# A decoder layer on one core: a quarter of the expert blocks' first layer moves beside the gate tables, and the window copies move forward

## The reference, cut to what matters

```python
def peer_ffn(x, wq, subkeys, u_tab, v_tab):          # x: 544 tokens of 1024
    q = (xi @ wq).reshape(PEER_TOKEN_BLOCK, PEER_HEADS, 2, PEER_DKEY // 2)
    s = jnp.einsum('nhcd,ckd->nhck', q, subkeys)      # 2 x 128 scores per head
    sv, si = lax.top_k(s, K)
    ...
    g = jax.nn.softmax(top_s, axis=-1)
    hpre = jnp.einsum('nd,nhkd->nhk', xi, u_tab[eid])
    a = jax.nn.gelu(hpre, approximate=False) * g
    return jnp.einsum('nhk,nhkd->nd', a, v_tab[eid])
...
kc = jnp.concatenate([state_k_win, kd_s], axis=1)     # k_win_sample: the window buffer moved on by 4 rows
vc = jnp.concatenate([state_v_win, vd_s], axis=1)
```

## Time and profile before

| | |
|---|---|
| median of 3 runs | 2651.59 us (2644.68 to 2654.73) |
| the profiled execution | 2648.93 us; its span 2647.1 us, mean granted clock 0.917 |
| busy over the span | PE 2289.9 us (87%), DVE 1610.1 (61%), ACT 928.9 (35%), POOL 359.4 (14%) |
| chain that ended last | PE 68%, DVE 10%, DMA 5% |
| transfers | 555 MB, mean 210 GB/s |

### The profile page before, as it was taken

The page is one execution under the profiler, slowest core; times in us unless marked ns, Lnnn a source line. Parts: engine busy times, 40 slices in busy tenths (PEclk is TensorE's granted clock), DMA queues, the critical chain, the costliest instruction groups (busy, mean ns, idle before and its releaser), DMA issues.

```text
span 2647.1 us, 38437 instructions
## 1 busy us (share of the span) xinstructions
PE 2289.9 (87%) x13177; PEld 1955.8 (74%) x13177; DVE 1610.1 (61%) x3159; ACT 928.9 (35%) x1417; POOL 359.4 (14%) x370
## 2 busy tenths in 40 slices
PE   7997879998997989504376999999999999999994
PEld 7996656666664469503376999999999999999993
DVE  3433322343434347799994667777677776777767
ACT  3225533444445122102263333333333333333331
POOL 0000000000000000100000223222232222322230
PEclk9998879899988989856687999999999999999997
DMA  3220026667665111299965888888787887878873
GB/s 121 91 73 33 1 91 200 201 207 225 198 201 190 64 48 49 80 323 339 364 263 201 278 274 283 275 281 278 272 284 275 282 278 273 285 273 282 278 273 105
DMA packets 214837, 555.47 MB, mean 210 GB/s; under 512 B 16993, under 2 KB 87202, under 8 KB 212066
## 3 DMA queue, kind: packets, MB, share of 16 engines
q1 hardware_dynamic: 165730, 315.16, 36.3%
q0 software_dynamic: 49024, 239.23, 25.4%
HBM read 521.95 MB, written 98.83 MB: 235 GB/s over the span
## 4 chain that ended last, share of the span: by engine, by line
PE 68%; DVE 10%; DMA 5%; SPq 2%; ACT 2%; issue 1%; POOLq 0%; DVEq 0%; ACTq 0%; POOL 0%
PE psum L1913 20%; PE psum L1925 19%; PE psum L1523 4%; PE psum L1903 4%; DMA gates_dram<-gate_table 3%; PE psum L978 3%; PE psum L1386 3%; PE psum L1050 2%; PE psum L1032 2%; DVE gate_table L1726 2%; PE psum L968 2%; PE psum L1000 2%; DMA sample<-in_cache_v_sb_dram 2%; DVE gate_table L1723 1%; PE psum L1766 1%
## 5 line engine op out<-in xcount | busy, mean ns | idle before, releaser
L1913 PE MATMUL psum<-h_parts,expert_parts 128*128 128x384 f32 x3072 | 592.9, 341 | 4.2 <-DVE expert_parts L2013 4.2
L1925 PE MATMUL psum<-expert_parts 128*128 128x512 f32 x2304 | 557.2, 395 | 0.0
L1913 PEld LDWEIGHTS psum<-h_parts,expert_parts 128*128 128x128 f32 x3072 | 537.7, 189 | 14.6 <-DVE expert_parts L2013 4.8
L1925 PEld LDWEIGHTS psum<-expert_parts 128*128 128x128 f32 x2304 | 423.3, 188 | 83.5
L2013 DVE TENSOR_TENSOR expert_parts<-psum,expert_parts 128x512 fp32r<-128x512 f32 x256 | 177.1, 692 | 293.2 <-ACT expert_parts L1955 293.2
L1961 ACT ACTIVATE expert_parts<-peer 128x1024 fp32r<-128x1024 f32 x128 | 135.8, 1061 | 365.9 <-PE psum L1925 365.9
L1955 ACT ACTIVATE expert_parts<-psum 128x512 fp32r<-128x512 f32 x256 | 153.1, 598 | 200.5 <-PE psum L1903 200.5
L2053 DVE SCALAR_TENSOR_TENSOR kept<-experts,kept 128x1024 f32<-128x1024 f32 x160 | 204.7, 1280 | 3.9 <-DVE kept L2043 2.8
L1305 DVE TENSOR_TENSOR sample_parts<-sample,sample_parts 128x512 fp32r<-128x512 f32 x128 | 85.2, 690 | 158.0 <-ACT sample_parts L1158 158.0
L394 PE MATMUL psum<-projection_parts 128*128 128x256 f32 (+1 forms) x1440 | 173.7, 282 | 3.8 <-DVE projection_parts L500 3.8
L1883 POOL DMA_INDIRECT experts<-in_peer_u_dram,kept x96 | 113.0, 1178 | 468.5 <-DVE experts L2037 345.4
(11 more groups left out here) (271 smaller groups left out, 2993.7 us busy)
## 6 DMA issues: line engine op xcount, KB each, us to landing
peer<-in_peer_u_dram SPq DMA_DIRECT2D x128, 512.0 KB, 5.6
peer<-in_peer_v_dram SPq DMA_DIRECT2D x128, 512.0 KB, 3.7
sample<-in_cache_k_sb_dram SPq DMA_DIRECT2D x128, 256.0 KB, 3.1
sample<-in_cache_v_sb_dram SPq DMA_DIRECT2D x128, 256.0 KB, 3.0
out_dram<-in_state_k_win_dram POOLq DMA_DIRECT2D x8, 4088.0 KB, 104.9
out_dram<-in_state_v_win_dram POOLq DMA_DIRECT2D x8, 4088.0 KB, 118.2
gates_dram<-gate_table SPq DMA_DIRECT2D x12, 2048.0 KB, 8.4
experts<-gates_dram SPq DMA_DIRECT2D x32, 768.0 KB, 6.0
```

Of the source, the lines that this page charges most:

```text
L1913: last = pe.matmul(bank(6)[:, 0:ND], lhsT=u_t[s][:, a, k, :], rhs=h1_r[:, b, k, 0:ND], start=(k == 0 and n == 0), stop=(k == KD - 1 and n ...
L1925: last = pe.matmul(bank(2 * t + half), lhsT=weight[s][:, a, t * P:(t + 1) * P], rhs=v_r[s][:, b, half * 512:(half + 1) * 512], start=(firs ...
```

## The change

1. **Early blocks.** Of every four expert blocks the last (block 4e+3, 32 in all) has its first layer computed in the gate-table stage, from the whole f32 tokens (`h1_f`, written by ACT in the norm stage by one more copy for each of six half tiles) and whole f32 `u`: per early block 8 transposes and 8 f32 matmuls on PE, two copies and a gelu on ACT, a load of 512 KB and a store of 192 KB (`gelu_dram`) on SP. Psum banks 6 and 7 hold them, so the table quarters go round three pairs of banks where they had four. 12 early blocks stand ahead of the first `turn`, 5 ahead of the second, 5 ahead of the third, and 10 inside chunks.
2. **Experts.** A block with k % 4 == 3 has no `turn_u`, `hidden` or `activate`; its gelu is loaded (L1996 of the changed kernel). SP issues the next `u` load ahead of the `v` load.
3. **Window copies.** The 16 copies are issued 7 in prompt attention (behind `counts_in`), 4 in dilated attention, 3 in the norm stage, 2 in the query stage.
4. **No barrier behind the queries**, and the query halves are 384 and 256 tokens wide instead of 320 each. The chunk loops of PE, ACT and SP are written out instead of looped.

```diff
+        MOVES = (7, 4, 3, 2)
+        def move_state(pool, turn):
+            for n in range(sum(MOVES[:turn]), sum(MOVES[:turn + 1])):
...
+                pool.dma_start(to[b].rearrange("w h d -> (w h d)")[0:(WIN - DT) * DH],
+                               frm[b].rearrange("w h d -> (w h d)")[DT * DH:WIN * DH]).then_inc(sem("window_moved"), 16)
...
         @part("pool")
         def _(pool):
+            pool.wait_ge(sem("counts_in"), 2 * 16)
+            move_state(pool, 0)
             pool.wait_ge(sem("v_sb_out"), 2 * 16)
...
+                    if t < NTD:
+                        act.activation(h1_f[:, 4 * half:4 * half + 4, t * P:(t + 1) * P],
+                                       bank(4 + u % 4).rearrange("p (k n) -> p k n", k=4), ACT.Copy)
...
-        for engine in programs:
-            programs[engine].append(end_stage)
...
+        EXP_AFTER = {1: 0, 5: 1, 10: 2, 15: 3, 22: 4}
+        BLOCK_OF = {1: 17, 2: 18, 3: 19, 4: 25, 5: 26, 6: 27, 7: 28, 8: 29, 9: 30, 10: 31}
+        FIRST_OF = ((0, 12), (12, 17), (20, 25))
+
+        def gate_schedule(turn, block, chunk):
+            for t in range(NTD + 1):
+                if t < NTD:
+                    for e in range(*FIRST_OF[t]):
+                        block(e)
+                    turn(t)
+                if t >= 1:
+                    for c in range(TILE_CHUNKS * (t - 1), TILE_CHUNKS * t):
+                        chunk(c, BLOCK_OF.get(c))
...
+            def hidden_early(e, half):
+                pe.wait_ge(sem("early_copied"), 2 * e + half + 1)
+                if half == 0 and e >= 1:
+                    pe.wait_ge(sem("early_gelu"), e)
...
+                for k in range(4 * half, 4 * half + 4):
+                    last = pe.matmul(bank(6)[:, 0:ND], lhsT=early_t[e % 2][:, k, :], rhs=h1_f[:, k, :],
+                                     start=(k == 0), stop=(k == KD - 1))
...
+            def block_half(e, half):
+                turn_early(e + 1, half)
+                hidden_early(e, half)
...
+            def exponents(e):
+                if e in EXP_AFTER:
+                    act.wait_ge(sem("best_less"), EXP_AFTER[e] + 1)
                     act.activation(gate_e, gate_e, ACT.Exp).then_inc(sem("gate_exp"), 1)
...
-                    for half in range(2):
-                        hidden(x, s, half)
-                        if not is_last(turn, k):
-                            turn_u(x + 1, 1 - s, SET * turn + (k + 1) // 2, half)
+                    if is_full(k):
+                        j = full_of(k)
+                        f = FULL * turn + j
+                        for half in range(2):
+                            hidden(f, j % 2, half)
+                            if not is_last(turn, k):
+                                turn_u(f + 1, 1 - j % 2, FULL // 2 * turn + (j + 1) // 2, half)
                     if not (isinstance(turn, int) and turn == 0 and k == 0):
                         add_up(x - 1, 1 - s, first=isinstance(turn, int) and turn == 0 and k == 1)
```

More of the change, by code:

```diff
@@ L681, in build, with _ @@
         assert place[0] <= WORK + 6 * WIDE
+        @part("pool")
+        def _(pool):
+            move_state(pool, 1)
         @part("pe")
@@ L1484, in top16, with _ @@
                 st.wait()
+        @part("pool")
+        def _(pool):
+            move_state(pool, 3)
         @part("sp")
@@ L1671, in build @@
         hot_i = [take(HALF_C * NK).rearrange("p (n i) -> p n i", n=HALF_C) for _ in range(2)]
[L1673 to L1677, removed]
+        early_gelu = [take(ND) for _ in range(2)]
+        early_t = [take(D).rearrange("p (k j) -> p k j", k=KD) for _ in range(2)]
         def columns(x, c, half, first=0, n=HALF_C):
@@ L1758, in turn, with turn_early @@
                 last.then_inc(sem("ijg_turn"), 1)
-            def spread(c, s, i):
+            def turn_early(e, half):
+                if e == SETS:
+                    return
+                if half == 0:
+                    pe.wait_ge(sem(f"early_in_{e % 2}"), 16 * (e // 2) + 16)
+                pe.wait_ge(sem("early_copied"), 2 * e + half)
+                for k in range(4):
+                    last = pe.transpose(bank(7)[:, k * P:(k + 1) * P], early_u[e % 2][:, 4 * half + k, :], ident)
+                last.then_inc(sem("early_turned"), 1)
@@ L1771, in _ @@
-            for t in range(NTD + 1):
-                if t < NTD:
-                    turn(t)
-                if t >= 1:
-                    pe.wait_ge(sem("ijg_turned"), min(t + 1, NTD))
-                    over_chunks(pe, t - 1, spread)
+                    for q in range(2 * half, 2 * half + 2):
+                        r = 4 * c + q
+                        pe.wait_ge(sem("table_copied"), r + 1)
+                        for n in range(QUARTER):
+                            at = q % 2 * QUARTER + n
+                            last = pe.matmul(bank(2 * (r % 3) + n // 4)[:, n % 4 * NK:(n % 4 + 1) * NK],
+                                             lhsT=hot_j[half][:, at, :], rhs=hot_i[half][:, at, :], start=True, stop=True)
+                        last.then_inc(sem("table_ready"), 1)
@@ L1778, in _ @@
+                    if e is not None:
+                        block_half(e, half)
+            turn_early(0, 0)
+            turn_early(0, 1)
+            gate_schedule(turn, block, chunk)
         @part("act")
         def _(act):
-            act.drain().then_inc(sem("table_copied"), 4)
+            act.drain().then_inc(sem("table_copied"), 3)
             act.drain().then_inc(sem("table_out_0"), 16)
             act.drain().then_inc(sem("table_out_1"), 16)
-            def copy(c, s, i):
-                act.wait_ge(sem(f"table_out_{s}"), 16 * i + 16)
-                for q in range(4):
-                    act.wait_ge(sem("table_ready"), 4 * c + q + 5)
-                    act.activation(table[s][:, :, 8 * q:8 * q + 8].rearrange("p i n -> p n i"),
-                                   bank(2 * q, 2).rearrange("p (n i) -> p n i", n=8), ACT.Copy).then_inc(sem("table_copied"), 1)
@@ L1804, in build @@
+            copy_early(0, 0)
+            copy_early(0, 1)
+            gate_schedule(turn, block, chunk)
+            gelu_early(SETS - 1)
         for engine in programs:
```

225 lines of the change are left out of this document (156 added, 69 removed).

## The result

The changed kernel takes **2499.9 us** (median of 4 runs, 2498.9 to 2501.6) where the kernel before took 2650.1 beside it: a ratio of 0.9435, 95% interval 0.9415 to 0.9454. The forecast was 2517 us, the range 2488 to 2560. The profiled execution took 2500.06 us, its span 2498.3, where 2647.1 stood before.

What follows compares the result with a forecast made beforehand. PE was taken to bound the experts, DVE the gate tables. Terms -160 + 1 + 5 + 19 + 1 = -134 us took the span from 2647.1 to 2513; adjusted to the median, 2517 us, range 2488 to 2560.

Steps and rivals of the forecast that it cites:

- experts: Expert stage: 32 blocks lose `hidden` and `turn_u`, 5.00 us each, if PE stays the bound: -160 us.
- gate tables: Gate tables: PE's early blocks fit nearly beside DVE's work, and copies no longer crowd table stores: +1 us, bounds -3 and +10.
- prompt attention, POOL's drain: Prompt attention: POOL's drain waits for seven copies, so the barrier opens at about 309 instead of 304: +5 us.
- norm stage: Norm stage: norm rows land only when three copies end, so PE stops 18 us, plus 1 for clock: +19 us.
- queries: Query stage: two copies hold the next piece of weights until about 981, some 6 us late: +1 us, bounds 0 and +6.
- rival C: Experts: the shortened block starves as `v_low` or its inputs come late: +16 to +48 us, 2533 to 2565; chance 0.12.
- SP gets 12 of its 16 turns while the copies last: Norm stage: queues alternate packet for packet, so the norm rows land when the copies end, about 911.5 to 912.5 us.
- Rival A: Norm stage: the norm rows are not held up by the copies, 19 us less, 2498 us; chance 0.17.
- The copies no longer crowd the table stores: Gate tables: DVE's 2.7 us wait for ACT, held up by a late-landing store, goes.
- The missing barrier gives no time: Start of the gate tables: DVE sets the pace and went straight on at 1110, so dropping the barrier gains nothing.
- 7 - 2.5 = 4.5 us: Gate tables, chunks 4 to 10: PE falls 7 us behind DVE; the double buffer of one-hot factors hides 2.5.
- Rivals B and D: Gate tables, PE's clock low: B at 0.76, +76 us, 2592, chance 0.10; D at 0.5 throughout, +268, 2785, chance 0.03.

Runs made afterwards that it cites:

- x6: The kernel before with the window copies moved 7, 4, 3, 2 and nothing else changed: 2665.1 us, ratio 1.0053.
- x5: The changed kernel with the barrier behind the queries put back: 2512.7 us, ratio 0.9479.
- x10: The changed kernel with the barrier back, ACT's first exponential ahead of the early blocks and the next three exponentials three early blocks earlier: 2508.5 us.
- x1: The changed kernel with six window copies in prompt attention and five in dilated attention: 2498.4 us, ratio 0.9428.
- x2: The changed kernel with POOL waiting for the norm's two rows before it issues the norm stage's three copies: 2491.1 us, ratio 0.9383.
- x3: The changed kernel with the norm's rows issued some 5 us later, behind two memsets of DVE, copies unmoved: 2515.4 us.
- x8: The changed kernel with copies split 6, 4, 5, 1 and those of the norm stage behind the norm's rows: 2479.7 us, ratio 0.9353.
- x4: The changed kernel with all 16 window copies in the gate tables again, early blocks kept: 2647.2 us, ratio 0.9991.

## Why the prediction was right, and where it was not

The forecast was right in sign and by its main term. Its sum was -134 us against -148.8 measured:

| term | forecast | measured | shown by |
|---|---|---|---|
| experts | -160 | -165.1 | changed, x6 |
| gate tables | +1 | -1.5 | x5, x6, x10 |
| prompt attention, POOL's drain | +5 | +6.4 | x1 |
| norm stage | +19 | +9.4 | x2, x3 |
| queries | +1 | +3.4 | x6, x8 |
| up to 204 us, dilated, sample, end | 0 | -1.4 | unedited |

**Experts.** The mechanism held: PE stayed the bound without a gap, so rival C did not come about. A block was 5.11 us cheaper, not 5.00: two runs of `add_up` that follow each other take 8.27 us (1911.24 to 1919.51) instead of 2 x 4.19; 32 x 5.11 = 163.5, and the rest is the stage's start, where PE's longest wait before the loop is 1.5 us instead of 2.7.

**Norm stage.** The mis-sized term. The step "SP gets 12 of its 16 turns while the copies last" took the two queues to start together. They share one for one, as I had read from the earlier trace rows, but half of the 256 row packets had gone before the copies' packets came. With the rows issued 5.6 us late the stage cost +22.8 (x3: 104.9 against 82.1); less those 5.6 us it is some 17 (an estimate), near the 19 of the forecast. Rival A's 2498 us is near the time by chance only: its premise, rows not held up, is false, since taking the hold away gives 9 us (x2).

**Gate tables.** Near in sum by luck: three parts were mis-sized, and they cancel. "The copies no longer crowd the table stores" was taken as 2.7 us and is 7.1 (x6). "The missing barrier gives no time" is false: it gives 12.8 us (x5), as PE's head start, and without it PE would hold DVE (x10). Of the early blocks themselves I had 7 - 2.5 = 4.5 us; with the barrier in place they cost 323.9 - 305.5 = 18.4 (x5 against x6), and only with the head start 5.6. PE's own work was sized well, 279 us busy where I had 281; what DVE pays for it was not. Rivals B and D did not come about: PE's longest wait in the stage was 4.8 us, and the clock was 0.96 to 0.98.

**Prompt attention and queries.** The drain ends when the copies do, as read from the earlier trace rows; the cost was 1.4 us larger. In the queries ACT waited for the late piece of weights, and PE for the low parts, 6.2 us instead of 3.7:

```profile
ACT wq_parts L1576 <- DMA peer<-in_peer_wq_dram: 10.9, 1, 10.9
...
PE psum L1562 <- DVE wq_parts L1610: 6.2, 2, 3.7
```

My estimate had the two copies end at 981 on the old time scale and PE covered by its pieces in hand; the cover was too thin by some 2 us, inside the bound of 6. The copies alone cost 1.2 us here (x6, halves of 320), and the new halves without the wait cost nothing (x8, 156.8 us against 157.1); why both together cost 3.4 is open.

## What to carry to other kernels

Work that moves off the engine that bounds a stage is worth its whole time if that engine stays without gaps, and its price lies where it goes. Look whether the engine there still has slack once the moved work is in; if not, a barrier ahead of it or an operation behind it on a third engine (here ACT's exponentials) becomes the price. A bulk copy was free here beside work that waits for no transfer (dilated attention took 69.0 to 71.3 us with four or five copies in it, 70.6 and 71.3 without) and dear beside small loads that something waits for: let the issuing engine wait for those loads first, and end the copies before the issuing engine's drain.

## What the runs showed of the hardware that was not expected

- Two queues go one packet for one, with 64 KB against 4 KB just as with 64 KB against 16 KB: 113 to 113 (880 to 900 us), 161 to 161 (x3) and 991 to 990 (x4, 160 us). A load of 4 KB rows that landed after 4.0 and 5.3 us alone (x2) took 27 to 38 us beside three copies (30.2 in the changed kernel, 27.1 and 37.9 in x3).
- SP's rows, issued 0.3 us before POOL's first copy, had moved 143 packets by 880 us when the copies had moved 15. How much of this lead comes from the 0.3 us and how much from how soon each queue starts behind its issue is not shown; no run took the lead away without also giving the copies one.
- SP itself stands while its queue is held: the two issues of query weights took 38.4 us on SP in the changed kernel and 1.09 us in x2 and x8, where the copies came later.
- POOL's drain in the barrier lasts until its copies are done: 91.4 us behind seven copies, 77.8 behind six.
